# A two-layer network with float32r matmuls: an unused gap of 1408 bytes ahead of the stage-wise tiles

## The chip, the cores and the metric

The kernel runs on one core of one Trainium2 chip. The metric is the device time of that core in microseconds (us), the median of the runs shown. All data is float32. TensorE is called PE here, VectorE DVE, ScalarE ACT, GpSimd POOL.

## What is computed

One sequence of 512 tokens with width 1024 goes through two blocks in a row. Every product `x @ w` below has a weight of 1024 x n or n x 1024 that is read from device memory once.

```python
# first block, layer 0: convolution module; layer 1: attention without softmax ("stick breaking")
h = (x @ pw1_a + b) * sigmoid(x @ pw1_g + b)         # 1024 -> 2 x 1024
h = silu(layer_norm(causal_dwconv31(h)))             # 31 taps along the tokens
mix = h @ pw2_w + pw2_b
# layer 1: q, k, v = x @ wq, x @ wk, x @ wv; mix = attention(q, k, v) @ wo
x = layer_norm(alpha * x + mix)
ffn = (silu(causal_dwconv3(x @ w_gate)) * (x @ w_up)) @ w_down   # 1024 -> 2816 -> 1024
x = layer_norm(alpha * x + ffn + sigmoid(x @ ple_gate) * (p @ ple_proj))
# second block: feed-forward, hybrid mixer (differential and sparse attention), feed-forward
x = x + 0.5 * rms_norm(swiglu(rms_norm(x)))
x = x + rms_norm(hybrid_mixer(rms_norm(x)))
x = x + 0.5 * rms_norm(swiglu(rms_norm(x)))
```

## The kernel before, in words

**Weights.** All weights lie in one array of 371 chunks of 128 x 1024. SyncE loads chunk after chunk into four slots of `raw` (L400). ACT rounds a chunk to float32r into `wH` (L1056), and POOL writes what the rounding left over, `raw - wH`, into `wL` (L419), which lies on the same bytes as `raw`. A slot is used again when PE has finished the chunk (`chunk_done`). Activations have two such parts too (`xH`, `xL` and so on), and each product is made of three matmuls: high times high, low times high, high times low.

**Two forms of product.** `tile_product` (L465, with `three`, L461 to L463) makes 128 outputs of all 512 tokens: a 128 x 128 piece of `wH` or `wL` is the stationary operand, and `xH` or `xL` with 512 columns moves. This form makes the gate/up stages (44 chunks each), the pointwise stage and the projections. `by_tokens` (L484) makes 128 tokens of 512 outputs: a 128 x 128 piece of the activation is stationary, and half a slot of `wH` or `wL`, 512 columns, moves:

```python
w = slice(half * S, half * S + S)
pe.matmul(bank, rh, wH[:, slot, w], start=start, stop=False)      # L487
pe.matmul(bank, rl, wH[:, slot, w], start=False, stop=False)      # L488
return pe.matmul(bank, rh, wL[:, slot, w], start=False, stop=stop) # L489
```

`full_product` calls it 8 times per chunk (4 token blocks, 2 halves), so 24 matmuls per chunk, and runs with `hH`, `hL` for the four down stages (22 chunks each), with `cH`, `cL` for `pw2` (8 chunks), `mH`, `mL` for `wo` (8), and `xH`, `xL` for `wout` (8). `project_p` runs it with `pH`, `pL` (2 chunks in each of two layers), and the gating stage of `ple` with `xH`, `xL` (8 chunks in each). Its last two chunks are done token block by token block (`last_chunks`, L549), so that the norm of a block (L1603, L1606, L1612 on DVE) starts while PE works on the next.

**Other PE work with the tiles concerned.** `conv_taps` (L684 to L686) does 8 of the 31 taps: `diagH` or `diagL`, a tap's weights on a diagonal, is stationary, and `gH` or `gL`, 512 columns that begin one element later for each tap, moves. `turn_block` (L498) turns a block of tokens with `turner` as the moving operand and `xr` or `tmp` as the stationary one. `cumulate` (L744) has `tri` stationary and `spH` or `spL` moving, 20 matmuls for each half of a head pair.

**Where tiles lie.** In each partition tiles are laid one behind another in the order in which they are made, each rounded up to 32 bytes. Counted from the first weight tile: `wL` (and `raw`) 0, `wH` 16384, `xr` 32768, `xH` 49152, `xL` 65536, `tmp` 81920, `b_row` 102400, `par` 106496, `con` 111040, `bcon` 116160, `tri` 116928, `st` 117952, `stat` 119104, which ends at 119424. That is 58 x 2048 + 640. There the `overlay` groups begin, which share the space behind it, one group for each kind of stage:

```python
hH, hL = overlay([("hH", [P, FT, S], F32R), ("hL", [P, FT, S], F32R)])
cH, cL = overlay([("cH", [P, KT, S], F32R), ("cL", [P, KT, S], F32R)])
```

A row of `hH`, `cH` or `mH` is 2048 bytes, so all of them, and `hL`, `cL`, `mL`, `pH`, `pL`, begin at 640 within 2048 bytes from the weights, and each token block 512 bytes further. `xH`, `xL`, `wH`, `wL` all begin at 0 within 2048 bytes. `turner` and `spH` begin at 640 too; `gH` at 896, `diagH` and `diagL` at 1408.

Of the kernel before, what the change touches and what calls it, by code (L numbers as in the profile page):

```python
# [12 lines left out]
P = 128  # L13
# [16 lines left out]
NEG = -1e30  # L30
SLOTS = 4
TAIL = 2
LEAD = SLOTS - 1
CMP_BLOCK = 32
CMP_STRIDE = 16
# [93 lines left out]
def build_block(nc, ws, xT, xN, pT, params, consts, rope, w1, rows, out):  # L129
    with ExitStack() as ctx:  # L130
        def sb(name, shape, dt=F32):
            return ctx.enter_context(nc.sbuf_tensor(name, shape, dt))
# [21 lines left out]
        rstd, vturn0 = b_row[:, 0:S], b_row[:, S:D]  # L154
        st = sb("st", [P, 288])
        stat = sb("stat", [P, 2, QT, 10])
        sq = [tmp[:, 8, :], tmp[:, 9, :]]
        g_row = tmp[:, 8:10, :].rearrange("p a b -> p (a b)")

# [297 lines left out]
        def _(pe):  # L457
# [75 lines left out]
            def full_product(name, nk, rH, rL, ready, ready_base, banks_free):  # L533
# [3 lines left out]
                def one_k(k, first=False):  # L537
                    pe.wait_ge(low_ready, c0 + k + 1)
                    pe.wait_ge(ready, ready_base + k + 1)
                    slot = (c0 + k) % SLOTS  # L540
                    for q in range(QT):
                        rh, rl = rH[:, k, q * P:q * P + P], rL[:, k, q * P:q * P + P]
                        for half in range(2):
                            if first:
                                banks_free(2 * q + half)
                            mm = by_tokens(ps[2 * q + half], slot, half, rh, rl, first, False)
                    mm.then_inc(chunk_done, 1)

                def last_chunks():  # L549
                    pe.wait_ge(low_ready, c0 + nk)  # L550
                    pe.wait_ge(ready, ready_base + nk)
                    for q in range(QT):
                        for k in range(nk - TAIL, nk):
                            t = slice(q * P, q * P + P)
# [7 lines left out]

                for k in range(nk - TAIL):
                    one_k(k, first=k == 0)
# [484 lines left out]
        def _(act):  # L1049
# [3 lines left out]
            def high(c, t=0):  # L1053

                act.wait_ge(raw_loaded[c % SLOTS], t * 16 + 16 * (c // SLOTS + 1))
                act.activation(wH[:, c % SLOTS, :], raw[:, c % SLOTS, :], ACT.Copy).then_inc(high_ready, 1)  # L1056

            def high_after(c, t=0):

                act.wait_ge(chunk_done, t * SLOTS + (c + 1))  # L1060
                high(c + LEAD, t)

            def highs(name):

                c0, n = CHUNK[name], dict(COUNTS)[name] - TAIL
                n = min(n, NCHUNKS - LEAD - c0)
                with act.Fori(0, n // SLOTS) as t:
# [9 lines left out]
            for n in range(KT):  # L1077
                act.wait_ge(x_loaded[n], 16)
                act.activation(xH[:, n, :], tmp[:, n, :], ACT.Copy).then_inc(x_high, 1)
            for c in range(2, LEAD):  # L1080
                high(c)
# [86 lines left out]
            def high_tiles(xname, h, lo, hi, shift=None, gain=None):  # L1168

                for b in range(lo, hi):  # L1170
                    act.wait_ge(x_turned, 8 * TURN[xname] + 4 * h + b + 1)
                    bank = ps[TURN_BANKS[xname][h][b]]
                    for n in (2 * b, 2 * b + 1):
                        if shift:
                            ins = act.activation(xH[:, n, HALF[h]], bank[:, HALF[n % 2]], ACT.Identity, bias=pc(shift, n))
                        else:
                            ins = act.activation(xH[:, n, HALF[h]], bank[:, HALF[n % 2]], ACT.Copy, scale=pc(gain, n))
                        ins.then_inc(x_high, 1)
# [12 lines left out]
            def mix_norm(layer):  # L1191
# [4 lines left out]
                def keep(q):  # L1196
                    if q < QT - 1:
                        act.wait_ge(proj_done, (QT - 1) * layer + q + 1)
                    else:
                        act.wait_ge(chunk_done, c0 + 2)  # L1200
                    act.activation(proj[:, q, :], banks[:, 2 * (q % 2):2 * (q % 2) + 2, :].rearrange("p a b -> p (a b)"),
                                   ACT.Copy).then_inc(proj_kept, 1)
# [10 lines left out]
                keep(1)  # L1213
                high(c0 + LEAD)
                high_tiles(xname, 0, 2, 4, shift=f"mix_b{layer}")
# [960 lines left out]
```

## Time and profile before

| | |
|---|---|
| median of 3 runs | 2453.79 us (2452.72 to 2454.97) |
| the profiled execution | 2452.42 us |
| its span, first to last instruction | 2450.6 us |
| mean granted clock of PE | 0.994 |
| PE busy | 2396.7 us (98%), 11435 matmuls |
| matmuls of L461 to L463 | 5928 |
| matmuls of L487 to L489 | 3168 |

PE matmuls are pipelined: one takes some 390 ns from start to end, but the next starts some 230 ns after it. So the busy time and the mean ns of a group tell little of PE's pace. The pace is the distance from one start to the next, which the timeline shows directly, and which a stretch shows by its count: a stretch counts every matmul that overlaps it, so a stretch of 100 us with n matmuls of 0.39 us has a spacing of (100 + 0.39) / n us. In a group, the tiles stand as "written <- moving, stationary".

### The profile page before, as it was taken

The page shows a single profiled execution, that of the slowest core. Times are in us where ns is not written, and L with a number is a line of the kernel's source. Part 1 is how long each engine was busy: PE and PEld are TensorE (multiplying, and loading weights), DVE is VectorE, ACT ScalarE, POOL GpSimd, SP SyncE. Part 2 cuts the span into 40 slices and gives each one's busy share as a digit, 9 for nine tenths or more (in the row PEclk, how much of TensorE's full clock was granted, in tenths as well). Part 3 has the DMA queues.
Part 4 walks back from the last instruction along what each step waited for, and adds up shares of the span by engine and source line. Part 5 has one row for each costly group of instructions (what it writes and reads, how often), then busy time and mean ns, then how long its engine had stood idle before and what let it go on. Part 6 is the DMA issues. An engine that isn't in the chain of part 4 may idle for free.

```text
span 2450.6 us, 30755 instructions
## 1 busy us (share of the span) xinstructions
PE 2396.7 (98%) x11435; PEld 1942.1 (79%) x11435; DVE 896.4 (37%) x1118; ACT 989.0 (40%) x1636; POOL 961.5 (39%) x422
## 2 busy tenths in 40 slices
PE   8989999999999999999999999999999989999998
PEld 6868888888877778888878888888877658888887
DVE  6985344420322214444410422210457862322201
ACT  7764333321566634433321622321434564322212
POOL 5834444444322214444444344444232102444443
PEclk9999999999999999999999999999999999999999
DMA  5112322222211112322222222222321102222222
GB/s 184 69 45 93 112 100 97 94 95 95 78 60 55 59 61 95 112 95 101 96 95 95 87 94 94 96 92 95 152 69 64 35 1 78 103 94 95 95 94 94
DMA packets 58756, 215.32 MB, mean 88 GB/s; under 512 B 6448, under 2 KB 6448, under 8 KB 58416
## 3 DMA queue, kind: packets, MB, share of 16 engines
q1 hardware_dynamic: 55440, 199.96, 23.6%
q10 hardware_dynamic: 3232, 14.16, 1.6%
q8 instruction: 63, 1.03, 0.2%
q14 instruction: 21, 0.17, 0.0%
HBM read 211.99 MB, written 2.10 MB: 87 GB/s over the span
## 4 chain that ended last, share of the span: by engine, by line
PE 89%; ACT 5%; DVE 4%; issue 1%; DMA 0%; SPq 0%; DVEq 0%; ACTq 0%
PE banks L461 17%; PE banks L463 17%; PE banks L462 17%; PE banks L487 9%; PE banks L488 9%; PE banks L489 9%; PE banks L498 1%; PE banks L744 1%; PE banks L860 1%; ACT lg L1331 1%; ACT lg L1333 1%; ACT spH L1342 1%; PE banks L731 1%; PE banks L755 1%; PE banks L903 1%
## 5 line engine op out<-in xcount | busy, mean ns | idle before, releaser
L419 POOL TENSOR_TENSOR wL<-raw,wH 128x1024 fp32r<-128x1024 f32 x369 | 898.3, 2436 | 1452.0 <-ACT wH L1056 1451.9
L1056 ACT ACTIVATE wH<-raw 128x1024 fp32r<-128x1024 f32 x371 | 393.1, 1060 | 1119.2 <-PE banks L463 607.6
L461 PE MATMUL banks<-xH,wH 128*128 128x512 f32 (+1 forms) x1976 | 762.6, 386 | 13.0 <-DVE xL L1567 10.6
L463 PE MATMUL banks<-xH,wL 128*128 128x512 f32 (+1 forms) x1976 | 756.5, 383 | 0.0
L462 PE MATMUL banks<-xL,wH 128*128 128x512 f32 (+1 forms) x1976 | 756.4, 383 | 0.0
L461 PEld LDWEIGHTS banks<-xH,wH 128*128 128x128 f32 x1976 | 372.1, 188 | 91.0 <-DVE wL L1572 10.6
L463 PEld LDWEIGHTS banks<-xH,wL 128*128 128x128 f32 x1976 | 372.0, 188 | 72.8
L462 PEld LDWEIGHTS banks<-xL,wH 128*128 128x128 f32 x1976 | 372.2, 188 | 71.8 <-issue 0.7
L487 PE MATMUL banks<-wH,hH 128*128 128x512 f32 x704 | 278.1, 395 | 3.5 <-DVE tmp L1681 3.5
L489 PE MATMUL banks<-wL,hH 128*128 128x512 f32 x704 | 277.8, 395 | 0.0
L488 PE MATMUL banks<-wH,hL 128*128 128x512 f32 x704 | 277.8, 395 | 0.0
L1683 DVE TENSOR_TENSOR hL<-tmp,hH 128x512 f32 x88 | 206.3, 2344 | 96.0 <-ACT hH L1262 96.0
L1681 DVE TENSOR_TENSOR tmp<-banks,tmp 128x512 f32<-128x512 f32 x88 | 60.9, 692 | 367.2 <-PE banks L463 354.5
L487 PEld LDWEIGHTS banks<-wH,hH 128*128 128x128 f32 x704 | 132.6, 188 | 35.9 <-issue 5.1
L489 PEld LDWEIGHTS banks<-wL,hH 128*128 128x128 f32 x704 | 132.6, 188 | 30.9
L488 PEld LDWEIGHTS banks<-wH,hL 128*128 128x128 f32 x704 | 132.6, 188 | 30.9
L1603 DVE SCALAR_TENSOR_TENSOR xr<-xr,banks 128x512 f32<-128x512 f32 x32 | 20.6, 681 | 266.7 <-PE banks L489 266.7
L1674 DVE SCALAR_TENSOR_TENSOR tmp<-banks,par,tmp 128x511 f32<-128x511 f32 x88 | 65.9, 749 | 139.3 <-ACT tmp L1252 132.6
L1627 DVE TENSOR_TENSOR banks<-banks,tmp 128x512 f32<-128x512 f32 x24 | 15.5, 692 | 264.5 <-ACT squares L1150 264.4
L1723 DVE SCALAR_TENSOR_TENSOR banks<-gpad,par,banks 128x512 f32<-128x512 f32 x112 | 75.1, 749 | 1.1 <-DVE tmp L1697 0.9
L487 PE MATMUL banks<-wH,xH 128*128 128x512 f32 x192 | 75.0, 391 | 0.0
L489 PE MATMUL banks<-wL,xH 128*128 128x512 f32 x192 | 74.7, 389 | 0.0
(248 smaller groups left out, 2397.2 us busy)
## 6 DMA issues: line engine op xcount, KB each, us to landing
raw<-ws SPq DMA_DIRECT2D x371, 512.0 KB, 3.2
w1b<-w ACTq DMA_DIRECT2D x2, 2048.0 KB, 11.4
tmp<-rows ACTq DMA_DIRECT2D x7, 512.0 KB, 4.3
b_row<-rows ACTq DMA_DIRECT2D x5, 512.0 KB, 4.6
tmp<-xT SPq DMA_DIRECT2D x8, 256.0 KB, 7.3
xr<-xN ACTq DMA_DIRECT2D x1, 2048.0 KB, 8.5
out<-xr SPq DMA_DIRECT2D x4, 512.0 KB, 2.6
pf<-pT ACTq DMA_DIRECT2D x2, 512.0 KB, 3.3
```

What stands on the lines that cost most here:

```text
L419: pool.tensor_tensor(wL[:, j, :], raw[:, j, :], fp(wH[:, j, :]), ALU.subtract).then_inc(low_ready, 1)
L461: pe.matmul(bank, wH[:, slot, cols], rh, start=start, stop=False)
L462: pe.matmul(bank, wH[:, slot, cols], rl, start=False, stop=False)
L463: return pe.matmul(bank, wL[:, slot, cols], rh, start=False, stop=stop)
L487: pe.matmul(bank, rh, wH[:, slot, w], start=start, stop=False)
L488: pe.matmul(bank, rl, wH[:, slot, w], start=False, stop=False)
L489: return pe.matmul(bank, rh, wL[:, slot, w], start=False, stop=stop)
L1056: act.activation(wH[:, c % SLOTS, :], raw[:, c % SLOTS, :], ACT.Copy).then_inc(high_ready, 1)
L1674: dve.scalar_tensor_tensor(tmp[:, j, back:S], ps[4 + 2 * j][:, 0:S - back], pc(f"fcw{inst}", f * FCONV_W + tap), tmp[:, j, back:S], ALU.mu ...
L1681: dve.tensor_tensor(tmp[:, 2 + j, :], ps[5 + 2 * j][:], tmp[:, j, :], ALU.mult).then_inc(h_made, 1)
L1683: dve.tensor_tensor(hL[:, bass.ds(f, 1), :].rearrange("p o t -> p (o t)"), tmp[:, 2 + j, :], fp(hH[:, bass.ds(f, 1), :].rearrange("p o t - ...
L1723: ins = dve.scalar_tensor_tensor(dst, g, w, sums[i % 2], ALU.mult, ALU.add)
```

## The change

One tile of 352 float32 (1408 bytes) per partition is made behind `stat` and never used. The overlay groups begin 1408 bytes further on, at 120832 = 59 x 2048 from the first weight tile, so `hH`, `hL`, `cH`, `cL`, `mH`, `mL`, `pH`, `pL`, `turner` and `spH` now begin at 0 within 2048 bytes. All tiles inside the groups keep their distances from each other. No instruction is added, removed or moved.

```diff
@@ -30,6 +30,7 @@
 SLOTS = 4
 TAIL = 2
+PAD = 352
 LEAD = SLOTS - 1
@@ -154,6 +155,7 @@
         st = sb("st", [P, 288])
         stat = sb("stat", [P, 2, QT, 10])
+        sb("pad", [P, PAD])
         sq = [tmp[:, 8, :], tmp[:, 9, :]]
```

## Rows read from the trace of the kernel before

**Rows 1.** The page: busy time by engine, and the chain that ended last.

```profile
PE 2396.7 (98%) x11435; PEld 1942.1 (79%) x11435; DVE 896.4 (37%) x1118; ACT 989.0 (40%) x1636; POOL 961.5 (39%) x422
...
PE 89%; ACT 5%; DVE 4%; issue 1%; DMA 0%; SPq 0%; DVEq 0%; ACTq 0%
```

**Rows 2.** Waits of PE: engine line waited for: us in total, times, longest us.

```profile
PE banks L461 <- DVE xL L1567: 10.6, 1, 10.6
...
PE banks L487 <- DVE tmp L1681: 3.5, 4, 0.9
```

**Rows 3.** PE in stretches: stretch, its length, PE busy (matmuls), clock, DMA share, GB/s.

```profile
176.00:206.00 30.00, 30.00 (x130) 1.00 0.34 125
400.00:500.00 100.00, 100.00 (x443) 1.00 0.28 96
530.00:630.00 100.00, 100.00 (x432) 1.00 0.27 95
901.00:931.00 30.00, 30.00 (x131) 1.00 0.30 105
...
2330.00:2430.00 100.00, 100.00 (x432) 1.00 0.26 90
```

**Rows 4.** Groups of PE by form: line, tiles (moving, stationary), count | busy us, mean ns.

```profile
L487 PE MATMUL banks<-wH,hH 128*128 128x512 f32 x704 | 278.1, 395 | 3.5 <-DVE tmp L1681 3.5
...
L487 PE MATMUL banks<-wH,mH 128*128 128x512 f32 x64 | 25.4, 396 | 0.0
L487 PE MATMUL banks<-wH,cH 128*128 128x512 f32 x64 | 25.4, 396 | 2.1 <-DVE cL L1589 2.1
...
L487 PE MATMUL banks<-wH,pH 128*128 128x512 f32 x32 | 12.8, 400 | 0.0
```

**Rows 5.** Timeline of PE in the first gating stage: start us, us, instruction.

```profile
244.70 0.39 PE L489 MATMUL banks<-wL,xH 128*128 128x512 f32 x1
...
247.42 0.39 PE L489 MATMUL banks<-wL,xH 128*128 128x512 f32 x1
```

**Rows 6.** Timeline of PE in the first down stage.

```profile
529.83 0.40 PE L488 MATMUL banks<-wH,hL 128*128 128x512 f32 x1
...
532.61 0.40 PE L488 MATMUL banks<-wH,hL 128*128 128x512 f32 x1
```

**Rows 7.** Timeline of PE, eight taps of the depthwise convolution.

```profile
68.15 0.39 PE L684 MATMUL banks<-gH,diagH 128*128 128x512 f32 x1
...
70.25 0.40 PE L684 MATMUL banks<-gH,diagH 128*128 128x512 f32 x1
70.49 0.39 PE L685 MATMUL banks<-gL,diagH 128*128 128x512 f32 x1
...
70.95 0.39 PE L684 MATMUL banks<-gH,diagH 128*128 128x512 f32 x1
71.17 0.40 PE L685 MATMUL banks<-gL,diagH 128*128 128x512 f32 x1
...
73.75 0.39 PE L461 MATMUL banks<-xH,wH 128*128 128x512 f32 x1
```

**Rows 8.** All engines in 20 us of gate/up and of down: busy us (instructions) PE, PEld, DVE, ACT, POOL.

```profile
420.00:440.00 20.00, 20.00 (x90) 16.58 (x89) 8.69 (x8) 7.27 (x10) 9.60 (x4) 1.00 0.31 105
560.00:580.00 20.00, 20.00 (x87) 16.20 (x86) 0.00 (x0) 3.20 (x4) 8.43 (x4) 1.00 0.25 88
```

**Rows 9.** Timeline of PE: one cumulate group of 20 matmuls, and the next instruction.

```profile
684.25 0.50 PE L744 MATMUL banks<-spH,tri 128*128 128x512 f32 x1 [0.35 <-DVE spL L1775]
...
687.06 0.44 PE L461 MATMUL banks<-xH,wH 128*128 128x512 f32 x1
```

**Rows 10.** Timeline of PE: the turning of one block.

```profile
231.22 1.95 PE L498 MATMUL banks<-turner,tmp 128*128 128x128 f32 x16
```

**Rows 11.** Timeline of PE and DVE at the end of the first down stage.

```profile
641.14 1.39 PE L498 MATMUL banks<-turner,tmp 128*128 128x128 f32 x11
...
642.01 0.68 DVE L1603 SCALAR_TENSOR_TENSOR xr<-xr,banks 128x512 f32<-128x512 f32 x1
```

## The prediction

> **What bounds the kernel now.** I read the page first: PE is busy for 98% of the span, and the chain that ended last lies on PE for 89% of it [rows 1]. The list of waits confirms it: the longest wait of PE, 10.6 us, is at the very start, and a down stage begins with a wait under 1 us [rows 2]. So wherever PE runs a long series of matmuls, the end moves by what each matmul costs, and no other engine has to be sped up with it.
>
> The next question is what one matmul costs. The reader is to look at the counts per stretch, since durations overlap [rows 3]. In gate/up, 400 to 500 us, 443 matmuls give (100 + 0.39)/443 = 226.6 ns from start to start. In a down stage, 530 to 630 us, 432 give 232.4 ns, and 2330 to 2430 us, in the last down stage, shows the same count. All of them have 512 moving columns, float32r, and the clock is 1.00 throughout. So the same amount of work costs 5.8 ns more. `pw2` with `cH` has (30 + 0.39)/130 = 233.8 ns, `wo` with `mH` has 232.0 ns [rows 3]. A stretch of 30 us is only good to one matmul in 130, some 1.8 ns.
>
> The two forms differ in which operand moves, so gate/up alone does not settle the cause. The timeline has a cleaner pair. In the gating stage the very lines of the down stage (L487 to L489) run with `xH` and `xL` stationary: from 244.70 to 247.42 us are 12 spacings, 226.7 ns each [rows 5]. With `hH` and `hL`, 12 spacings take 2.78 us, 231.7 ns each [rows 6]. Form, moving tile, shape and clock are the same. What differs is where the stationary tile lies: `xH` at 0 within 2048 bytes from the weights, `hH` at 640. I take it that the load of the next weights and the moving stream of the running matmul disturb each other at some distances between their addresses and not at others.
>
> The convolution's taps speak for addresses in a second way. There the moving tile begins 4 bytes later with each tap, and the spacing is not constant: 240 ns from 70.25 to 70.49 us, 220 ns from 70.95 to 71.17 us (good to 10 ns), 5.60/24 = 233.3 ns in the mean over all 24 [rows 7]. These tiles lie behind `hH`'s start, so a fast spacing does occur in that part of the memory.
>
> **The change, part by part.** It issues nothing, waits for nothing and moves no step. Every term is a count times a difference in spacing.
>
> 1. Down stages: L487 ran 704 times with `hH` [rows 4], three lines make 2112 matmuls. 2112 x (232.4 - 226.6 = 5.8 ns) = 12.2 us. After the change `hH` stands to `wH` as `xH` does, a multiple of 2048 bytes; the eight rows of `xH` cover eight such multiples at one price.
> 2. `pw2`: 3 x 64 = 192 matmuls [rows 4] x (233.8 - 226.6) = 1.4 us.
> 3. `wo`: 192 x (232.0 - 226.6) = 1.0 us.
> 4. `project_p`: 3 x 32 = 96 [rows 4] x 5.8 = 0.56 us. Half of these products run while PE would wait for the norm anyway, so I take 0.3 us.
> 5. The ends of the long products. A token block of the last two chunks is 12 matmuls, 2.79 us, and would be 2.72. DVE is already late there: PE has finished the last block and starts to turn at 641.14, while DVE starts on that block at 642.01 [rows 11]. What PE gains in the last three blocks, 3 x 0.07 us, is then waited for again. Over six such ends that is up to 1.3 us; some of it remains, since the turning starts at once, so I give back 0.5 us.
>
> The sum is -12.2 - 1.4 - 1.0 - 0.3 + 0.5 = -14.4 us.
>
> **What must keep up.** With 24 matmuls a chunk will take 5.44 us instead of 5.58. Gate/up already runs at that pace with more beside it: in 20 us ACT is busy 7.27, DVE 8.69 and POOL 9.60 us, against 3.20, 0 and 8.43 in the down stage [rows 8]. So a faster PE meets no new bound, and the weight loads are at 105 GB/s there without holding PE up.
>
> **What the trace does not price.** Three groups of PE work also get another distance, to tiles that do not move or by absolute address, and no row shows them at it.
> - `cumulate`, 16 groups of 20 matmuls; one group takes 684.25 to 687.06, 2.81 us [rows 9]. `spH` moves against `tri`. Bounded by the one known difference, 5.8 ns for each of 320 matmuls: -1.9 to +1.9 us. I take 0, because neither the distances of now (`spH` 448 bytes behind and 64 before the two halves of `tri`, within 2048) nor those of then (192 and 704 before) are those of a row that I can read.
> - `turner`: 16 turns took 1.95 us with the 0.28 us of the last, 111 ns each [rows 10]; 384 in all, -2.2 to +2.2 us by the same bound. I take 0: they have 128 columns, and only part of them is on the path.
> - The convolution: `gH` and `diagH` shift together, so their distance stays. If the absolute start mattered, 192 matmuls could go from 233.3 to 226.6 or to the slowest spacing, 240: -1.3 to +1.3 us [rows 7]. I take 0.
> The other tiles of the groups shift together or are read by engines that wait for PE.
>
> The profiled execution took 2452.42 us, so it would be 2438.0; it stands 1.37 us under the median of the runs. Off that median, 2453.79 - 14.4 = 2439.4 us.
>
> **Rivals.**
> - *The same work, no gain, because it is not the offset.* The cause could be the place of the tile (all slow ones lie 119424 bytes from the weights or further, all fast ones within 81920) or something else that goes with it. For it: no row shows a fast product with an upper tile of the same form. Against it: the spacings of 220 ns in rows 7, which belong to tiles 123776 bytes from the weights and further. Time 2453.8 us. Chance 0.04.
> - *Loads and stream never meet.* What the rows show is a spacing that depends on the stationary tile, 231.7 against 226.7 ns [rows 5, 6], with nothing waited for. If the two reads cannot disturb each other, this difference has another source, and moving the tile changes nothing: 2453.8 us. Chance 0.03, since two products that differ in nothing but that tile differ by 5 ns. The Trainium skill states such a rule, in "SBUF — State Buffer", section "Who interferes with whom": PE has two independent read ports, one for the moving operand and one for the weights, and "PE and ACT never wait on anyone". By that rule the change is worth 0; the trace does not agree with it here, if my reading of the rows is right.
> - *Half of it.* `cH` and `mH` lie on the same bytes and still show 233.8 and 232.0 ns [rows 3], so the spacing depends on history as well, on the phase in which a stage begins. A stage could settle between the two, near 229.5 ns: 2592 x 2.9 ns = 7.5 us, 2446.3 us. Against it: the aligned rows are at 226.6 and 226.7 in two forms. Chance 0.06.
> - *Slower.* The distance of 0 is a bad one for this size of tile, or the phase locks where load and stream meet each time. The price is the slowest spacing in the trace, 240 ns [rows 7]: 2592 x (240 - 232.4) = +19.7 us, 2473.5 us. It decides from a spacing of 234.3 ns in the down stages on. For it: the convolution shows that some distances cost more than 640 does. Against it: `xH` is at distance 0 and at the fast end. Chance 0.03.
>
> **How the numbers follow.** The forecast has 0.84. That the change does not do what it says is part of the first rival: if the tiles did not land at 59 x 2048, nothing would come of it. Within the forecast, the unpriced groups can move the time by some 5 us down if all gain and as much up; they hardly all go one way, so I take 4 down and 3 up, 2435.4 to 2442.4, and reach on to 2446.6 to hold the half case. The measurement of this kernel tells 0.2%, 4.9 us, from no change. Faster than that (below 2448.9): forecast and half case, less a little, 0.89. Within it: the two cases of no effect and the rest, 0.08. Slower: 0.03.
>
> **What would show it.** In the profile after, a stretch of 100 us in each down stage counts 443 matmuls instead of 432, and the 12 spacings of a down stage take 2.72 us. L487 with `hH` has a mean near 390 ns instead of 395 [rows 4]. Stages between them keep their lengths: gate/up 443 per 100 us, the convolution's pattern of taps as it was. Each down stage is some 3 us shorter. The forecast is wrong if a down stage still counts 432, or if it counts 443 and the time does not follow, which would mean that DVE or the loads set the pace at its end.

## The result, and the profile after

The changed kernel takes 2438.0 us (median of 6 runs, 2435.63 to 2439.6) against 2453.67 us (6 runs of the kernel before). The ratio is 0.9937, 95% interval 0.9926 to 0.9947: faster by 15.7 us, 0.6%. The profiled execution took 2438.68 us, 13.7 us less than the profiled one of before; how far the clock moves such a single execution is told below.

The page of the changed kernel, to be read against [rows 1]. Lines of the code stand two further down, so L487 is now L489.

```profile
span 2436.9 us, 30755 instructions
...
PE 2380.1 (98%) x11435; PEld 1938.3 (80%) x11435; DVE 897.2 (37%) x1118; ACT 988.8 (41%) x1636; POOL 959.6 (39%) x422
```

The count of instructions on each engine is the same, and so is the work of DVE, ACT and POOL within 2 us. PE lost 16.6 us of busy time.

PE in stretches (columns as in [rows 3]):

```profile
176.00:206.00 30.00, 30.00 (x134) 1.00 0.40 138
400.00:500.00 100.00, 100.00 (x443) 1.00 0.27 94
530.00:630.00 100.00, 100.00 (x443) 1.00 0.28 95
901.00:931.00 30.00, 30.00 (x134) 1.00 0.35 119
2330.00:2430.00 100.00, 100.00 (x442) 1.00 0.25 87
```

The down stages at 530 and 2330 now count 443 and 442 in 100 us, where [rows 3] had 432: (100 + 0.39)/443 = 226.6 ns from start to start, the same as gate/up at 400. `pw2` (176) and `wo` (901) count 134 in 30 us, 226.8 ns, where 130 and 131 stood.

The timeline of PE in the first down stage, first and last row of 12 spacings:

```profile
529.65 0.39 PE L491 MATMUL banks<-wL,hH 128*128 128x512 f32 x1
...
532.37 0.39 PE L491 MATMUL banks<-wL,hH 128*128 128x512 f32 x1
```

These are 2.72 us, 226.7 ns each, against 231.7 in [rows 6]. The groups by form, busy us and mean ns, for `hH` and `cH`:

```profile
L489 PE MATMUL banks<-wH,hH 128*128 128x512 f32 x704 | 274.4, 390 | 3.5 <-DVE tmp L1683 3.5
...
L489 PE MATMUL banks<-wH,cH 128*128 128x512 f32 x64 | 25.0, 391 | 2.1 <-DVE cL L1591 2.1
```

They fell from 395 and 396 ns to 390 and 391 [rows 4], as much as the spacing.

**Where the time went, stage by stage.** Each number is the difference in the distance between the first and the last start of a stage in the two timelines. Four down stages: 122.54 us became 119.56, 119.56, 119.54 and 119.54, together -12.0 us. `pw2` with the first `project_p` product behind it -1.4, `wo` with its own -1.15, the second `project_p` product of each layer -0.12 each, -0.24 together. Gating, `wout` and all four gate/up stages: within 0.02 each. That is -14.8 us from the faster spacing. The rest, +1.0 us, is -0.7 in the stage up to `pw2`, -1.8 in the attention, +3.1 in the hybrid mixer and +0.45 in the norm and turning ahead of the last two gate/up stages (0.20 of it behind the second down stage, which comes with the change: step 3 below). The first three are stages with small pieces of work, where PE's granted clock falls now and then to 1.2 GHz, mostly in or just behind a pause of PE of 2.5 to 3.3 us, and not at the same places in every run. The same two stretches in the kernel before and then after, all engines, clock in the third column from the end:

```profile
860.00:900.00 40.00, 36.55 (x199) 26.71 (x198) 8.81 (x12) 18.12 (x26) 4.12 (x2) 0.91 0.15 47
1738.00:2024.00 286.00, 271.21 (x1636) 203.55 (x1636) 184.14 (x320) 137.77 (x358) 57.47 (x24) 0.98 0.17 62
```

```profile
857.00:897.00 40.00, 35.29 (x207) 25.37 (x206) 8.81 (x12) 19.18 (x27) 5.21 (x3) 1.00 0.17 57
1723.00:2012.00 289.00, 272.82 (x1633) 204.92 (x1634) 185.53 (x321) 138.81 (x361) 57.44 (x24) 0.96 0.17 62
```

The clock of the last head pair's stretch was 0.91 before and 1.00 after; in the hybrid mixer it was 0.98 before and 0.96 after. PE had 1.2 GHz there for 13.7 us before and for 20.5 us after, and the mixer took 3.1 us longer in this execution. The gap is not to blame: of the seven runs below with down stages as fast as these, six have a mixer between 1.9 us shorter and 0.3 us longer than the kernel before (286.3 to 288.5 us against 288.2), and the seventh (`convalign`, 291.2 us) has 20.5 us at 1.2 GHz in it as well. So single executions scatter by 2 to 4 us, in the stages in which the clock falls, and the stages, not the totals, are what to compare.

**A view that misleads.** The chain that ended last, [rows 1] before, now reads:

```profile
issue 47%; PE 24%; POOL 20%; DVE 5%; ACT 2%; DMA 1%; POOLq 0%; SPq 0%; DVEq 0%; ACTq 0%
```

It looks as if PE had lost the lead to POOL. It has not: PE has no more idle time in the long stages than before, its waits are the same within 0.2 us but for 1.4 us in `cumulate` (7.2 against 5.8 us), and run `off32`, which is as slow as the kernel before, shows 47% issue and 20% POOL too, while `off768`, as fast as the change, shows PE 84%. The chain follows inferred releasers back from the end and can change to another branch early; from there on it stays with it. Counts and starts do not depend on that.

### The profile page after: what moved, and what is told of

It reads as the page before. It is cut to its first block, busy times and chain, and to the rows that moved or that the text cites. A ratio compares the mean times of both kernels' runs of the same rounds, so it can differ in the third digit from the quotient of the medians.

```text
span 2436.9 us, 30755 instructions
## 1 busy us (share of the span) xinstructions
PE 2380.1 (98%) x11435; PEld 1938.3 (80%) x11435; DVE 897.2 (37%) x1118; ACT 988.8 (41%) x1636; POOL 959.6 (39%) x422
## 4 chain that ended last, share of the span: by engine, by line
issue 47%; PE 24%; POOL 20%; DVE 5%; ACT 2%; DMA 1%; POOLq 0%; SPq 0%; DVEq 0%; ACTq 0%
POOL wL L421 20%; PE banks L463 5%; PE banks L464 5%; PE banks L465 5%; DVE banks L1725 3%; PE banks L489 2%; PE banks L491 2%; PE banks L490 2%; PE banks L862 1%; PE banks L905 1%; ACT tmp L1490 1%; DMA raw<-ws 1%; PE banks L817 0%; DVE st L1921 0%; DVE tmp L1957 0%
## 5 line engine op out<-in xcount | busy, mean ns | idle before, releaser
L489 PE MATMUL banks<-wH,hH 128*128 128x512 f32 x704 | 274.4, 390 | 3.5 <-DVE tmp L1683 3.5
L490 PE MATMUL banks<-wH,hL 128*128 128x512 f32 x704 | 274.1, 389 | 0.0
L491 PE MATMUL banks<-wL,hH 128*128 128x512 f32 x704 | 274.1, 389 | 0.0
L489 PEld LDWEIGHTS banks<-wH,hH 128*128 128x128 f32 x704 | 132.2, 188 | 32.1 <-issue 5.1
L491 PEld LDWEIGHTS banks<-wL,hH 128*128 128x128 f32 x704 | 132.2, 188 | 27.6
L490 PEld LDWEIGHTS banks<-wH,hL 128*128 128x128 f32 x704 | 132.2, 188 | 27.1
L489 PE MATMUL banks<-wH,xH 128*128 128x512 f32 x192 | 75.0, 391 | 0.0
L491 PE MATMUL banks<-wL,xH 128*128 128x512 f32 x192 | 74.8, 389 | 0.0
```

## The experiments

The kernels of one group shared a chip with a run of the kernel before, and are compared with that one. Spacings are worked out from the counts of 100 us, as above.

### 1. Which distance: 1024, 768, 32 bytes

The theory of the prediction: the distance between the tile whose weights are loaded and the tile that streams decides, and place does not. Rivals: any gap helps, or the place in the memory decides.

```diff
-PAD = 352      # changed kernel, 1408 bytes
+PAD = 96       # off1024
+PAD = 32       # off768
+PAD = 360      # off32
```

> The gap is 384 bytes instead of 1408, so the stage tiles begin at 1024 within 2048 bytes from the weights. Theory A (only the distance within 512 bytes counts, since token blocks 512 bytes apart already cost the same): down stages at 226.7 ns from start to start, time within 2 us of the changed kernel, some 2438. Theory B (the distance within 2048 bytes counts, as the change says): at least one token block is at a slow distance and the mean stays over 229 ns, time 2446 or more. Theory C (any gap helps, place and not distance): fast.

> The gap is 128 bytes, the tiles begin at 768 within 2048, 256 within 512. Theory A (distance within 512 bytes): slow, 230 to 234 ns in the down stages, time 2448 to 2458; if the period were 256 or 128 bytes it would be 226.7 ns and 2438. Theory B (within 2048): slow as well. Theory C (any gap helps): fast, 2438.

> The gap is 1440 bytes, the tiles begin 32 bytes behind the aligned place. If exact alignment is needed: above 229 ns in the down stages, time above 2445. If the disturbance needs a distance of more than a few tens of bytes: 226.7 ns, 2438. The convolution, whose moving tile shifts by 4 bytes a tap and whose spacing goes from 225 to 243 ns, speaks for the first.

Gate/up (400) and down (530) in `off1024`, `off768` and `off32`:

```profile
400.00:500.00 100.00, 100.00 (x443) 1.00 0.28 95
530.00:630.00 100.00, 100.00 (x443) 1.00 0.29 100
```

```profile
400.00:500.00 100.00, 100.00 (x443) 1.00 0.28 96
530.00:630.00 100.00, 100.00 (x443) 1.00 0.28 95
```

```profile
400.00:500.00 100.00, 100.00 (x443) 1.00 0.29 97
530.00:630.00 100.00, 100.00 (x430) 1.00 0.29 95
```

`off1024` took 2436.52 us and `off768` 2434.7, with the kernel before at 2450.86 on that chip: both have the full gain. `off32` has 430 matmuls in 100 us, 233.5 ns, and took 2453.49 us. So a gap as such does nothing, and exact alignment is needed, at least down to 32 bytes. That 768 is fast went against theory A as against theory B, which both expected a slow run, and was only an aside of A: the distance counts within 256 bytes, not within 512 or 2048.

### 2. The kernel before's own distance at another place: 896, and 64

```diff
-PAD = 352
+PAD = 64       # off896
+PAD = 368      # off64
```

> The gap is 256 bytes, the tiles begin at 896 within 2048, which is 128 within 256, as 640 is. If the spacing follows the distance within 256 bytes: the down stages at 232.4 ns with the pattern of the kernel before, each stage 122.5 us, time 2450 to 2455. If 640 itself was bad, or the period is 512 bytes and only some distances cost: another spacing, down to 226.7 ns and 2437.

> The gap is 1472 bytes, the tiles begin 64 bytes behind the aligned place. 32 bytes gave 233.3 ns and 128 bytes 232.4 ns. If every distance other than a multiple of 256 bytes costs: 232 to 234 ns, time 2450 to 2456. If the period is 64 bytes (32 slow, 64 fast) it would be 226.7 ns; against that stand the 128 of the kernel before.

The first and the last down stage in `off896`, then gate/up and down in `off64`:

```profile
530.00:630.00 100.00, 100.00 (x430) 1.00 0.28 95
2330.00:2430.00 100.00, 100.00 (x432) 1.00 0.27 90
```

```profile
400.00:500.00 100.00, 100.00 (x443) 1.00 0.30 100
530.00:630.00 100.00, 100.00 (x430) 1.00 0.28 95
```

896 bytes is 128 within 256, as 640 is, and it costs the same: 2452.23 us against 2452.62 of the kernel before. 64 bytes is slow as well, 2454.13. With 0 (three times), 32, 64 and 128 (twice), the distances tried within 256 bytes for these products are: 0 fast, all others slow.

`off896` shows one thing more. Its first down stage counts 430 (233.5 ns), its last 432 (232.4 ns), with the same addresses. The starts show two patterns that repeat exactly: one of seven spacings from 228 to 241 ns, mean 232.4, and one of two, 229 and 238 ns, mean 233.3. A stage falls into one of them and stays. That is what separated `cH` (233.8) from `mH` (232.0) in [rows 3]. In `off32` and `off64` all four down stages show the pattern of two, at 231 and 235 ns and at 230 and 236 ns, with the same mean of 233.3; the pattern of seven was seen only at 128 bytes.

### 3. The lower tiles made slow

If place decided, `xH` and `xL` would stay fast wherever they lie in the lower part.

```diff
         xr = sb("xr", [P, QT, D])
+        sb("gap1", [P, 160])
         xH = sb("xH", [P, KT, S], F32R)
         xL = sb("xL", [P, KT, S], F32R)
+        sb("gap2", [P, 352])
```

> The kernel before, with 640 bytes ahead of xH and 1408 behind xL: only xH and xL move, to 640 within 2048 bytes, and stay in the lower part of the memory; hH stays at 640. Distance theory: the gating and wout stages (xH stationary) go from 226.8 to 232.4 ns, gate/up (xH moving) from 226.6 to 230 to 234 ns; with 6120 matmuls the time rises by 20 to 45 us, to 2475 to 2500. Place theory (upper tiles slow, lower fast): no difference, 2454.

Gate/up and down, then two groups of PE by form, gate/up's and the gating stages':

```profile
400.00:500.00 100.00, 100.00 (x432) 1.00 0.28 94
530.00:630.00 100.00, 100.00 (x432) 1.00 0.28 94
```

```profile
L464 PE MATMUL banks<-xL,wH 128*128 128x512 f32 x1848 | 729.8, 395 | 0.0
...
L489 PE MATMUL banks<-wH,xH 128*128 128x512 f32 x192 | 76.0, 396 | 0.0
```

Gate/up, where `xH` streams, fell from 443 to 432 matmuls in 100 us; its group of low parts has a mean of 395 ns where the kernel before had 390, and the gating group is at 396, 391 before. Down, which was not touched, is at 432 as before. The time rose by 24.2 us to 2475.09, from 2450.86 on that chip. The four gate/up stages are 5.7 to 6.0 us longer each, gating and `wout` 1.1 us each; the stage up to `pw2`, where DVE sets the pace (experiment 6), is not longer. The rule holds with either tile as the moving one, and the place is out.

The same run bounds the rule. The attention has matmuls of the same form with 256 moving columns. Two starts in `xshift`, 9 spacings apart:

```profile
655.49 0.28 PE L465 MATMUL banks<-xH,wL 128*128 128x256 f32 x1
...
656.56 0.28 PE L465 MATMUL banks<-xH,wL 128*128 128x256 f32 x1
```

These are 119 ns each, and the kernel before, with `xH` at distance 0, has 120 ns. In this form a distance of 128 bytes costs nothing at 256 columns.

### 4. Distance or absolute address

```diff
+        sb("front", [P, 160])     # allshift; [P, 8] in allshift32
         raw, = overlay([("raw", [P, SLOTS, 1024], F32)])
```

> The changed kernel with 640 bytes more ahead of all tiles, so every distance between tiles is as in the changed kernel and every absolute address is 640 further. If the distance between the two operands counts: all stages as in the changed kernel, 226.7 ns in down and in gate/up, time 2434 to 2440. If the absolute start of a tile counts: all long stages at 232 to 233 ns, 8700 matmuls, some 2490.

> The changed kernel with 32 bytes ahead of all tiles: every distance as in the changed kernel, every absolute address 32 bytes further. If only the distance between the operands counts, down to 32 bytes: 226.7 ns in down and gate/up, 2434 to 2440. If the absolute start counts within 128 bytes, which a shift by 640 bytes could not show and which would explain why the convolution's taps stay slow at matched distances: above 229 ns in both forms, over 2455.

Gate/up and down in `allshift` and in `allshift32`:

```profile
400.00:500.00 100.00, 100.00 (x443) 1.00 0.28 94
530.00:630.00 100.00, 100.00 (x443) 1.00 0.30 99
```

```profile
400.00:500.00 100.00, 100.00 (x443) 1.00 0.29 94
530.00:630.00 100.00, 100.00 (x443) 1.00 0.29 97
```

Both are fully fast, 2436.3 and 2436.11 us against 2452.62 and 2454.47 of the kernel before. Where all tiles lie together does not matter, by 640 bytes nor by 32; how they stand to each other does.

### 5. One slow load in three

```diff
-        hH, hL = overlay([("hH", [P, FT, S], F32R), ("hL", [P, FT, S], F32R)])
+        hH, _, hL = overlay([("hH", [P, FT, S], F32R), ("hgap", [P, 160], F32), ("hL", [P, FT, S], F32R)])
```

> The changed kernel with 640 bytes between hH and hL, so that in the down stages one of the three weight loads (hL) is at the slow distance. If each load pays by itself: a third of the cost, 228.6 ns, each down stage 120.5 us, time 2441. If one slow load upsets the phase of the next ones too: over 230 ns, 2445 or more. If it is absorbed by the two fast ones: 226.7 ns, 2437.

Gate/up and down, and four starts from the timeline of the down stage:

```profile
400.00:500.00 100.00, 100.00 (x443) 1.00 0.28 94
530.00:630.00 100.00, 100.00 (x434) 1.00 0.28 95
```

```profile
559.80 0.39 PE L491 MATMUL banks<-wL,hH 128*128 128x512 f32 x1
560.02 0.40 PE L489 MATMUL banks<-wH,hH 128*128 128x512 f32 x1
560.26 0.40 PE L490 MATMUL banks<-wH,hL 128*128 128x512 f32 x1
560.49 0.39 PE L491 MATMUL banks<-wL,hH 128*128 128x512 f32 x1
```

Down counts 434, 231.3 ns, and the time is 2445.17 against 2452.62 us; each down stage takes 121.88 us, so 0.66 of the 2.98 us are kept. In the mean over a stage, the spacing behind L489 (`hH` works, `hL` is loaded) is 232.7 ns, that behind L490 (`hL` works, `hH` is loaded) 234.0, that behind L491 226.7. So the matmul under which `hL` is loaded pays, and the one after it too; the third is free. One load in three at the slow distance costs nearly four fifths of three, and the second of the expectations holds. The trace does not show which of the two reads is held up: the rows of the loads themselves last 188, 192 and 188 ns behind the three starts, and 188 ns in the stages of either kernel, fast or slow.

### 6. Can the convolution have it too?

Here the moving tile starts 4 bytes further with each tap, so each tap's diagonal was put 516 bytes behind the last, at the tap's own distance of 0 within 256. The gap is 128 bytes, and the same gap was timed alone beside it.

```diff
+        ROW, DIAG = 576, 1088
...
-            ("gpad", [P, 2, GP], F32), ("gH", [P, 2, GP], F32R),
-            ("gL", [P, 2, GP], F32R), ("diagH", [P, 2, PE_TAPS, P], F32R), ("diagL", [P, 2, PE_TAPS, P], F32R),
+            ("gpad", [P, 2, ROW], F32), ("gH", [P, 2, ROW], F32R),
+            ("gL", [P, 2, ROW], F32R), ("diagH", [P, 2, DIAG], F32R), ("diagL", [P, 2, DIAG], F32R),
...
+        gpad, gH, gL = (t[:, :, 0:GP] for t in (gpad, gH, gL))
+        diagH, diagL = (t[:, :, 0:PE_TAPS * (P + 1)].rearrange("p j (t c) -> p j t c", c=P + 1)[:, :, :, 0:P]
+                        for t in (diagH, diagL))
```

> The gap of 128 bytes again, timed. If a distance that is a multiple of 256 bytes is all that matters, it is worth what the 1408 bytes are: ratio to the kernel before 0.9937 within 0.001, 2436 to 2440. If the 1408 bytes do something beyond it, the ratio is nearer to 1.

> The gap of 128 bytes, and in the convolution the rows of gpad, gH and gL are 2304 bytes and each tap's diagonal lies 516 bytes behind the last, so that the diagonal of a tap starts at a multiple of 256 bytes from the moving tile of that tap, which itself starts 4 bytes later each time. If the distance is the rule and not the absolute start: two of three loads are exact and one is off by 4 bytes, and the 24 matmuls of a channel tile take 5.45 to 5.50 us instead of 5.59. If a moving start off its line costs by itself: 5.59 still. In time either way within 1.5 us of the gap alone, since DVE is busy 98% of that stage.

PE's timeline in `convalign`, the first start of 24, two in the middle, and the next product's first; then all engines in the convolution stage:

```profile
67.75 0.39 PE L690 MATMUL banks<-gH,diagH 128*128 128x512 f32 x1
...
71.69 0.40 PE L692 MATMUL banks<-gH,diagL 128*128 128x512 f32 x1
71.93 0.39 PE L690 MATMUL banks<-gH,diagH 128*128 128x512 f32 x1
...
73.32 0.39 PE L467 MATMUL banks<-xH,wH 128*128 128x512 f32 x1
```

```profile
60.00:130.00 70.00, 70.00 (x307) 57.53 (x307) 68.94 (x94) 51.75 (x118) 55.45 (x36) 1.00 0.19 62
```

The 24 matmuls take 5.57 us instead of 5.59 or 5.60, and spacings of 240 ns are still there. The first expectation, 5.45 to 5.50, is wrong. Why is not settled, and two causes remain. One is a load at a slow distance: the next tap's `diagH` is loaded while this tap's `gH` moves, 4 bytes off, which is one load in three. `hLoff` showed that one in three keeps 78% of the whole cost; by that share the 24 matmuls would take 5.44 + 0.78 x (5.59 - 5.44) = 5.56 us (an estimate), close to the 5.57. Against it: `hLoff` has a free spacing of 226.7 ns in each three, and here the means behind L690, L691 and L692 are 230.6, 232.4 and 233.4 ns. The other is the start of the moving tile, some multiples of 4 bytes off its row. `allshift32` shows that an absolute shift by 32 bytes is free, so if the absolute start matters it does so below 32 bytes. No run separates the two: the tiles' starts are rounded to 32. In time it is worth nothing either, as DVE is busy 68.94 of 70 us there: ratio 0.9936 (0.9922 to 0.9949).

The gap of 128 bytes alone has 2436.77 us (5 runs) and a ratio of 0.9938 (0.9924 to 0.9952): the change with 1280 bytes less. No version tried is measurably faster than the changed kernel.

### 7. `tri` at the rule's distance

```diff
-PAD = 352
+PAD = 272
...
+        sb("tripad", [P, 80])
         tri = sb("tri", [P, 2, P], F32R)
```

> The changed kernel with 320 of the gap's 1408 bytes moved ahead of tri, so that spH and spL stand at a multiple of 256 bytes from tri and everything behind as in the changed kernel. If the distance rule holds for cumulate too: the first two matmuls of a group at 227 instead of 229 to 232 ns, a head pair's 40 matmuls 0.1 to 0.2 us shorter than 6.04 us. If the weight loads of the short matmuls set the pace there: no change. In time under 1.5 us either way.

Timeline of PE, the first group of a head pair: its first three starts, 0.23 us apart, and its last.

```profile
677.03 0.39 PE L747 MATMUL banks<-spH,tri 128*128 128x512 f32 x1
677.26 0.39 PE L747 MATMUL banks<-spL,tri 128*128 128x512 f32 x1
677.49 0.33 PE L747 MATMUL banks<-spH,tri 128*128 128x384 f32 x1
...
679.62 0.28 PE L747 MATMUL banks<-spL,tri 128*128 128x128 f32 x1
```

In such groups, which begin without a wait, the first two spacings went to 226 and 227 ns from 229 and 232 in the changed kernel, and from 235 and 235 in the kernel before. So the rule holds there as well, with `tri` as the stationary tile; within 256 bytes `tri` stood 64 bytes behind `spH` before and 192 behind it after the change. This half of the first expectation came true, the other did not: a head pair's 40 matmuls took 6.03 to 6.06 us instead of 6.04 to 6.05. The gain of some 10 ns in two of 40 matmuls is lost in that scatter. The time was 2436.8 us. That the weight loads set the pace of the short matmuls was not tried.

## Why the prediction was right

The forecast was 2439.4 us, and 2438.0 was measured; the range was 2435.4 to 2446.6. By its steps:

1. *Down stages, 12.2 us.* Measured 12.0. The spacing went to 226.7 ns, as `xH` has it.
2. *`pw2` 1.4, `wo` 1.0, `project_p` 0.3.* Measured 1.2, 1.0 and 0.5. The counts of 30 us were good to 0.2 us for `pw2`, whose spacing was 233.3 ns and not 233.8. `project_p` was halved for a wait on the norm, and there is none: the turning follows each product at once in both kernels, and the four products gained 0.16, 0.13, 0.12 and 0.12 us. The two misses cancel.
3. *The ends, 0.5 us given back.* DVE now starts on the last block 1.07 us after PE has begun to turn, 0.87 before [rows 11]:

```profile
635.96 2.28 PE L500 MATMUL banks<-turner,tmp 128*128 128x128 f32 x19
...
637.03 0.68 DVE L1605 SCALAR_TENSOR_TENSOR xr<-xr,banks 128x512 f32<-128x512 f32 x1
```

   So the 0.2 us that PE gained in the last three blocks are waited for, as said. The norm and turning behind the second down stage took 0.20 us longer, and 0.18 to 0.20 in six other runs with fast down stages (in `convalign` the clock fell there). Behind the first and the third the clock's scatter covers it. The term was right in kind; its size of 0.5 us in all could not be told.
4. *`cumulate`, `turner` and the convolution at 0, within some 5 us.* `cumulate` went from 6.06 to 6.04 us for a head pair, under 0.2 us in all; the turns took 3.49 us for 32 before and after; 24 taps took 5.59 and 5.60 us, where 5.59 and 5.61 stood. The zeros were right, the bounds far too wide. `turner` too moved to a distance of 0, and its 112 ns did not change, so the distance does not set its pace.
5. *Half-clock stretches* were in no term. With them the rest of the profiled execution is 1.0 us longer, the 0.2 us of step 3 included, so its 13.7 us are less than the 14.8 us of the stages. The median's 15.7 us are more than either. The change itself is worth some 14.6 us by the stages, against 14.4 forecast; that the forecast lies 1.4 us from the measured median is the scatter of the runs.

What was not quite right is the rule behind it. The prediction took the distance within 2048 bytes, as the change does. It is 256 bytes (experiments 1 and 2); that token blocks 512 bytes apart had one price already spoke for a shorter period. For this change both give the same number.

The rivals: *not the offset* fell with `off32` and `xshift`, since a gap alone does nothing and lower tiles can be made slow. *Loads and stream never meet* fell with the aligned runs, and `hLoff` shows it load by load: with `hL` alone at the slow distance, the matmul under which it is loaded and the next one are slower, by 6.0 and 7.3 ns. So the rule of the Trainium skill, in "SBUF — State Buffer", section "Who interferes with whom", that PE's two reads go through independent ports and that PE never waits on anyone, does not agree with the trace here: the distance between the two costs 5.8 of 232.4 ns. About other engines no run here says anything. By what means the two reads disturb each other, a shared bank or something else, is not shown; only addresses were varied. *Half of it* rested on a sound reading, since the spacing does depend on how a stage begins, but only at slow distances: aligned, the down stages have 226.7 ns in the mean, and `pw2`, `wo` and `project_p` 226.6 to 227.1 ns, one longer spacing of some 310 to 340 ns left out where a stage has it. *Slower* did not come: 0 is the best of the distances tried.

## What to carry to other kernels

Where float32r matmuls with 512 columns follow each other without a wait, each loading new weights, count the starts per 100 us in each stage. If stages of one shape differ by 2 to 3%, compare the start addresses of the stationary and the moving tile within 256 bytes, and put them at the same one with a gap; rows whose length is a multiple of 64 float32 (256 bytes) keep it by themselves. With 256 columns it brought nothing here (119 ns off the line, 120 on it). It pays only where PE sets the pace; look for that in PE's waits and idle time, and not in the chain alone.

## What the runs showed that was not expected

- The period is 256 bytes: 768 and 1024 from the weights are as fast as 2048, and 32, 64 and 128 within 256 all cost 5.7 to 6.6 ns per matmul of 512 columns. Matmuls of 256 columns pay nothing at 128 (`xshift`).
- At a distance of 128 bytes there are two patterns of spacing, 232.4 and 233.3 ns in the mean, and a stage may fall into either at the same addresses and keeps it (`off896`: 430 and 432 per 100 us), worth 0.5 us in a stage of 528 matmuls.
- One slow load in three costs 78% of what three cost (121.88 against 119.56 and 122.54 us).
- A moving tile that starts 4 bytes further per tap stays at 232 ns even when each tap's diagonal is set to its distance (5.57 us for 24). Whether the one load in three that is 4 bytes off does it, or the start itself, is open.
